# Moving the S5 rotation phases from GpSimd to ScalarE and VectorE in a two-layer SSD/S5 kernel

## The reference, cut to what matters

```python
for i in range(DEPTH):                       # DEPTH = 2
    u = rmsnorm(h, mix_norm_w[i])
    mix = ssd_mixer(u, ...) if i % 2 == 0 else s5_mixer(u, ...)
    h = h + mix
    h = h + conv_ffn(rmsnorm(h, ffn_norm_w[i]), ...)     # up 1024->5632, 3 taps, silu*val, down 2816->1024
    h = h + per_layer_embed(h, p[i], ...)                # (p @ w_proj) * sigmoid(rmsnorm(h) @ w_gate)
return rmsnorm(h, final_norm_w)
```

```python
step = jnp.exp(log_step[d])[:, None]
mag = jnp.exp(lr * step)
ang = li * step
lb_re = mag * jnp.cos(ang)
lb_im = mag * jnp.sin(ang)
```

## Time and profile before

| | |
|---|---|
| median of 3 runs | 1598.86 us (1595.52 to 1599.97) |
| the profiled execution | 1595.06 us |
| its span, first to last instruction | 1593.3 us |
| TensorE busy | 1517.2 us, 95% |
| VectorE busy | 1177.2 us, 74% |
| ScalarE busy | 725.6 us, 46% |
| GpSimd busy | 242.8 us, 15% |
| mean granted TensorE clock | 0.971 |

### The profile page before, as it was taken

How to read it: one execution, slowest core, us unless ns; L and a number is a source line. 1 busy time by engine, 2 the same in 40 slices (tenths; PEclk the granted TensorE clock), 3 DMA queues, 4 the chain that set the end, 5 groups by cost and what they waited for, 6 DMA issues and landing times.

```text
span 1593.3 us, 20269 instructions
## 1 busy us (share of the span) xinstructions
PE 1517.2 (95%) x7383; PEld 1233.8 (77%) x7383; DVE 1177.2 (74%) x1362; ACT 725.6 (46%) x1104; POOL 242.8 (15%) x244
## 2 busy tenths in 40 slices
PE   7989999999989999999998979989999999999998
PEld 5757767777677788888876759988888888888886
DVE  5687768678787989979899878974676666743354
ACT  4554454545634555224445451423355555532244
POOL 0154212020116600030057110000100000001001
PEclk9989999999999999999999995979999999999999
DMA  4334225234214433543335587932323323323222
GB/s 142 86 122 133 80 66 160 66 124 138 83 53 93 130 112 127 203 154 119 132 106 204 185 304 240 314 90 93 96 89 95 103 92 101 110 86 99 86 93 86
DMA packets 192234, 199.01 MB, mean 125 GB/s; under 512 B 47886, under 2 KB 178526, under 8 KB 188062
## 3 DMA queue, kind: packets, MB, share of 16 engines
q1 hardware_dynamic: 184510, 192.76, 38.1%
q10 hardware_dynamic: 7648, 5.25, 1.1%
HBM read 169.47 MB, written 28.51 MB: 124 GB/s over the span
## 4 chain that ended last, share of the span: by engine, by line
PE 72%; DVE 17%; issue 5%; DMA 2%; ACT 2%; SPq 0%; POOL 0%; DVEq 0%; ACTq 0%
PE ring L2111 21%; PE ring L2121 21%; PE ring L2112 21%; DVE w_lo L1483 2%; DVE rb L1893 2%; PE ring L2377 1%; DVE cc L1605 1%; PE pe_s L2397 1%; PE ring L2262 1%; DMA w_raw<-in_ssd_w_out 1%; DVE ytmp L1779 1%; DVE zs L1785 1%; DVE fwd L1643 1%; PE pe_s L2132 1%; ACT w_hi L1050 1%
## 5 line engine op out<-in xcount | busy, mean ns | idle before, releaser
L2111 PE MATMUL ring<-uh,w_hi 128*128 128x512 f32 x1160 | 458.8, 395 | 11.6 <-DVE cc L1605 3.7
L2112 PE MATMUL ring<-ul,w_hi 128*128 128x512 f32 x1160 | 453.8, 391 | 0.0
L1050 ACT ACTIVATE w_hi<-w_raw 128x1024 fp32r<-128x1024 f32 (+1 forms) x233 | 239.5, 1028 | 434.1 <-PE ring L2112 347.2
L1483 DVE TENSOR_TENSOR w_lo<-w_raw,w_hi 128x1024 fp32r<-128x1024 f32 (+1 forms) x233 | 287.5, 1234 | 163.6 <-PE ring L2121 139.8
L2121 PE MATMUL ring<-uh,w_lo 128*128 128x512 f32 x1160 | 288.7, 391 | 6.3 <-DVE w_lo L1483 6.3
L2111 PEld LDWEIGHTS ring<-uh,w_hi 128*128 128x128 f32 x1160 | 218.9, 189 | 64.2 <-issue 10.7
L2121 PEld LDWEIGHTS ring<-uh,w_lo 128*128 128x128 f32 x1160 | 218.0, 188 | 53.5 <-DVE w_lo L1483 7.8
L2112 PEld LDWEIGHTS ring<-ul,w_hi 128*128 128x128 f32 x1160 | 218.8, 189 | 47.2 <-issue 1.6
L2111 PE MATMUL ring<-gh,w_hi 128*128 128x512 f32 x480 | 189.2, 394 | 4.1 <-ACT w_hi L1050 2.8
L2112 PE MATMUL ring<-gl,w_hi 128*128 128x512 f32 x480 | 188.1, 392 | 0.0
L1992 DVE SCALAR_TENSOR_TENSOR cc<-cin,par,cc 128x512 f32<-128x512 f32 x176 | 129.6, 799 | 1.0 <-ACT cc L1406 1.0
(11 more groups left out here) (343 smaller groups left out, 2038.2 us busy)
## 6 DMA issues: line engine op xcount, KB each, us to landing
w_raw<-in_ffn_w_up SPq DMA_DIRECT2D x88, 512.0 KB, 3.5
w_raw<-in_ffn_w_down SPq DMA_DIRECT2D x40, 512.0 KB, 3.4
w_raw<-in_ssd_w_in SPq DMA_DIRECT2D x32, 512.0 KB, 3.8
s_tables<-tab SPq DMA_DIRECT2D x16, 1024.0 KB, 4.7
slot<-s_tables SPq DMA_DIRECT2D x16, 1024.0 KB, 7.3
fwd<-log_decays SPq DMA_DIRECT2D x16, 512.0 KB, 5.0
w_raw<-in_ssd_w_out SPq DMA_DIRECT2D x16, 512.0 KB, 3.5
w_raw<-in_ple_w_gate SPq DMA_DIRECT2D x16, 512.0 KB, 3.5
```

The source lines that it names most:

```text
L1050: act.activation(w_hi[u % 2][:, 0:n], w_raw[:, u % 2, 0:n], ACT.Copy).then_inc(hi_done, 1)
L1483: dve.tensor_tensor(w_lo[u % 2][:, 0:n], w_raw[:, u % 2, 0:n], w_hi[u % 2][:, 0:n].bitcast(F32), ALU.subtract).then_inc(lo_done, 1)
L2111: pe.matmul(o, wh[:, k, c], rh[:, k0 + k, :], start=first and k == 0, stop=False)
L2112: mm_ = pe.matmul(o, wh[:, k, c], rl[:, k0 + k, :], start=False, stop=False)
```

## The change

The four GpSimd steps of a turn are replaced. ScalarE makes the phase, eight scaled copies of the 64 multiples, one per group (128x64 each, the scale read from a column), and then adds the rounding constant in one 128x512 Identity with a bias column. VectorE subtracts the constant and the phase in one scalar_tensor_tensor of 128x512, which gives the difference with its sign turned; the sine's scale is negated for that. On ScalarE the turns of a round stand between the round's `hi_to` and its `squares`; the sines follow one round later, and the last two stand behind the square root. SyncE's saves of the turns stand behind D7, D8, D10, D11, then two behind P1, and the rest as before. Apart from that, the low half of F4 in the first pair of both FFNs is made ahead of its taps.

```diff
--- before.py
+++ after.py
@@ -279,7 +279,7 @@
         turn_at = [turn_a[:], turn_b[:], cin[:, :, 2:2 + SEQ], cc[:, 2:4, :],
                    ffn0[2][:].rearrange("p b n -> p (b n)").rearrange("p (a n) -> p a n", a=2)]
         turn_at += turn_at[0:3]
-        steps_row, quarter = tri[:, 0, 0:NCH], tri[:, 1, 0:1]
+        steps_row, quarter, magic = tri[:, 0, 0:NCH], tri[:, 1, 0:1], tri[:, 1, 1:2]
         bq_tmp = ct[:, 0]
         pv = ct[:, 1].rearrange("p g h -> p (g h)").rearrange("p (a n g) -> p a n g", a=2, n=LC)
         pv_tmp = ct[:, 0].rearrange("p g h -> p (g h)")[:, 0:(LC - 1) * S5G].rearrange("p (n g) -> p n g", g=S5G)
@@ -746,7 +746,7 @@
                                 saved = ({0: 1, 4: 2, 5: 3, 8: 4, 10: 5}, {2: 10, 7: 11, 10: 12})[part].get(n * i + kg)
                                 if saved is not None:
                                     save_table(saved)
-                                turned = {5: 0, 6: 1, 8: 2, 9: 3, 11: 4}.get(part * (n * i + kg))
+                                turned = {7: 0, 8: 1, 10: 2, 11: 3}.get(part * (n * i + kg))
                                 if turned is not None:
                                     turn_save(turned)
                 u = U[("ple", layer)]
@@ -763,6 +763,7 @@
                             proj_load(i)
                         if layer == 0:
                             if (i, kg) == (0, 0):
+                                turn_save(4)
                                 turn_save(5)
                             if (i, kg) == (0, 1):
                                 turn_save(6)
@@ -951,32 +952,13 @@
             def s5_steps():
                 pool.memset(tri[:, 0, 0:1], 0.0).then_inc(steps_done, 1)
                 pool.memset(quarter, PI / 2.0).then_inc(steps_done, 1)
+                pool.memset(magic, ROUND_MAGIC).then_inc(steps_done, 1)
                 for n in range(6):
                     w = 1 << n
-                    pool.wait_ge(steps_done, n + 2)
+                    pool.wait_ge(steps_done, n + 3)
                     pool.tensor_scalar(tri[:, 0, w:2 * w], tri[:, 0, 0:w], float(w), None, ALU.add, ALU.bypass
                                        ).then_inc(steps_done, 1)
-                pool.wait_ge(steps_done, 8)
-
-            def s5_turns(n):
-                if n < 2:
-                    pool.wait_ge(unit_done, U[("up", 0, 1)])
-                elif n < 4:
-                    pool.wait_ge(f_gl, HT + 2)
-                elif n == 4:
-                    pool.wait_ge(filled, FILL[("p", 0)] + PK)
-                else:
-                    pool.wait_ge(t_saved[n - 5], 16)
-                x, r = (turn_at[n][:, a].rearrange("p (g k) -> p g k", g=GB) for a in range(2))
-                pool.tensor_tensor(x, steps_row.unsqueeze(1).to_broadcast([P, GB, NCH]),
-                                   v5[:, V_F, GB * n:GB * n + GB].unsqueeze(2).to_broadcast([P, GB, NCH]), ALU.mult
-                                   ).then_inc(t_step, 1)
-                pool.wait_ge(t_step, 4 * n + 1)
-                pool.tensor_scalar(r, x, ROUND_MAGIC, None, ALU.add, ALU.bypass).then_inc(t_step, 1)
-                pool.wait_ge(t_step, 4 * n + 2)
-                pool.tensor_scalar(r, r, -ROUND_MAGIC, None, ALU.add, ALU.bypass).then_inc(t_step, 1)
-                pool.wait_ge(t_step, 4 * n + 3)
-                pool.tensor_tensor(r, x, r, ALU.subtract).then_inc(t_step, 1)
+                pool.wait_ge(steps_done, 9)
 
             def cut_rows(n):
 
@@ -1016,12 +998,8 @@
             pool.wait_ge(pv_done, 8)
             s5_order(ptv, lambda rows, a: pv[rows, a], ptv_done, (1.0, 1.0))
             pool.wait_ge(ptv_done, 4)
-            for n in range(5):
-                s5_turns(n)
             for m in range(1, KD - 2):
                 add_square(2, m)
-                if m in (1, 3, 5):
-                    s5_turns(5 + m // 2)
             for m in range(1, KD - 2):
                 add_square(3, m)
             pool.wait_ge(unit_done, U[("ple", 0)] + 12)
@@ -1381,14 +1359,32 @@
                 std(1 + 3 * layer)
                 if layer == 0:
 
+                    def turns(n):
+
+                        if n == 0:
+                            act.wait_ge(steps_done, 9)
+                            act.wait_ge(unit_done, U[("up", 0, 1)])
+                        elif n == 2:
+                            act.wait_ge(f_gl, HT + 2)
+                        elif n == 4:
+                            act.wait_ge(filled, FILL[("p", 0)] + PK)
+                        elif n > 4:
+                            act.wait_ge(t_saved[n - 5], 16)
+                        x, r_ = (turn_at[n][:, a] for a in range(2))
+                        for g in range(GB):
+                            act.activation(x[:, NCH * g:NCH * g + NCH], steps_row, ACT.Copy,
+                                           scale=v5[:, V_F, GB * n + g:GB * n + g + 1]).then_inc(t_step, 1)
+                        act.wait_ge(t_step, (GB + 1) * n + GB)
+                        act.activation(r_, x, ACT.Identity, bias=magic).then_inc(t_step, 1)
+
                     def sines(n):
 
                         x, r_ = (turn_at[n][:, a] for a in range(2))
-                        act.wait_ge(t_step, 4 * n + 4)
+                        act.wait_ge(steps_done, 9 + n + 1)
                         act.activation(x, r_, ACT.Abs).then_inc(t_abs, 1)
                         act.wait_ge(t_abs, n + 1)
                         act.activation(x, x, ACT.Sin, scale=-TURN, bias=quarter).then_inc(t_sin, 1)
-                        act.activation(r_, r_, ACT.Sin, scale=TURN).then_inc(t_sin, 1)
+                        act.activation(r_, r_, ACT.Sin, scale=-TURN).then_inc(t_sin, 1)
 
                 r = 2 + 3 * layer
                 for part, (first, pairs) in enumerate(parts):
@@ -1436,17 +1432,23 @@
                     for i in range(4):
                         hi_to(u + n * i + n + 1)
                         if part == len(parts) - 1:
+                            if layer == 0:
+                                turns(2 * i)
+                                turns(2 * i + 1)
                             if (layer, i) == (0, 0):
                                 act.wait_ge(tab_op, 6 * NB)
                             for m in (2 * i, 2 * i + 1):
                                 squares(r, m)
                                 u_hi(r, m, UH[layer])
-                            if layer == 0:
-                                sines(2 * i)
-                                sines(2 * i + 1)
+                            if layer == 0 and i:
+                                sines(2 * i - 2)
+                                sines(2 * i - 1)
                 u = U[("ple", layer)]
                 hi_to(u + 2)
                 std(r)
+                if layer == 0:
+                    sines(6)
+                    sines(7)
                 for i in range(4):
                     hi_to(u + GATE[i] + 3)
                     if layer == 1 and i >= 2:
@@ -1980,8 +1982,7 @@
                             for j in range(2):
                                 dve.tensor_tensor(cin[:, j, 2:2 + SEQ], bank(t + 2 * half + j), rstd[:], ALU.mult
                                                   ).then_inc(evac, 1)
-                            if not mixed:
-                                lo(u + 2 * half + 3, at=i * 4)
+                            lo(u + 4 if mixed else u + 2 * half + 3, at=i * 4)
                             for tap in range(1, 3):
                                 for j in range(2):
                                     if tap == 1:
@@ -1994,7 +1995,8 @@
                                                              scalar=dcol(i * 2 + (C_FCW + c)), in1=cc[:, 2 * half + j, :],
                                                              op0=ALU.mult, op1=ALU.add).then_inc(f_taps, 1)
                             if half == 0:
-                                lo(u + 4, at=i * 4)
+                                if not mixed:
+                                    lo(u + 4, at=i * 4)
                                 tables(more and more - 1)
                         for j in range(2):
                             dve.wait_ge(f_silu, i * 2 + (done + j + 1))
@@ -2043,6 +2045,12 @@
                         if part == len(parts) - 1:
                             for m in (2 * i, 2 * i + 1):
                                 u_lo(r, m, UH[layer], UL[layer])
+                            if layer == 0:
+                                for b in (2 * i, 2 * i + 1):
+                                    x, r_ = (turn_at[b][:, a] for a in range(2))
+                                    dve.wait_ge(t_step, (GB + 1) * (b + 1))
+                                    dve.scalar_tensor_tensor(out=r_, in0=r_, scalar=-ROUND_MAGIC, in1=x, op0=ALU.add,
+                                                             op1=ALU.subtract).then_inc(steps_done, 1)
 
                 u = U[("ple", layer)]
                 lo_to(u + 2)
```

## The result

The changed kernel takes 1627.63 us (median of 4 runs, 1621.28 to 1628.22) against 1599.41 before (4 runs, 1595.52 to 1600.34): ratio 1.0168, 95% interval 1.0146 to 1.0190, **28 us slower**. The prediction was 1622, range 1606 to 1633.

A forecast was written before the change was run, and what follows sets the result against it. TensorE, 95% busy, was taken as the bound, so edits count only through its waits. 23.7 + 1 = 24.7 us on 1595.06 gave 1619.8, 1623.6 with the median's 3.8; it said 1622, range 1606 to 1633.

The forecast's parts named there:

- Round 0 gains: With GpSimd's turns gone, D3's wait goes: at most 6.4 us of idle and some 2 us of slow clock back.
- ScalarE's block: Turns, squares, high halves and sines on ScalarE take 11.4 us a round instead of 5.9, uncovered in later rounds.
- The exposed loads: SyncE's loads for D8, D11, P2, P3 wait behind saves; a full load takes 4.6 us, a half one 3.6.
- TensorE's waits: Waits for high halves: some 8 us before D8, 6 to 8 before D11, 9 before P2, 6 before P3.
- P3's high half: At the PLE, done at 908.4 against 884.66 before, 23.7 us later; the order behind it is the old one.
- two signs of being wrong: Wrong if ScalarE reaches D8's high half before 846, or if D8's load is issued before 842.
- The table load ahead of sine 6: A second table load on ScalarE, back to the sine behind the square root, costs 1.28 us.
- F4: First FFN, low half ahead of the taps: the wait moves to F5, +1 us, between -3 and +3.
- B: Rival: blocks lengthen but loads are found in time, saves not holding them; +11 us, 1609; chance 0.11.
- C: Rival: blocks hide in ScalarE's waits, only VectorE's relief is left; 8 us less, 1591 or 1587; chance 0.09.
- D: Rival: the gain and the cost balance, 1599 us; chance 0.05.
- E: Rival: saves right ahead of loads stretch these to 6 us and more, with slow clock; +35, 1634; chance 0.07.

The follow-up runs named there:

- e7: The kernel before with GpSimd's four steps of a turn replaced by one fill, phases not computed: 1591.42 us, ratio 0.9958.
- e1: The changed kernel with every save of a turn one weight load later in SyncE's queue: 1616.52 us, ratio 1.0085 to the kernel before.
- e4: The kernel before, GpSimd's turns kept, only sines and saves reordered as in the change: 1615.61 us, ratio 1.0087.
- e5: The changed kernel with F4's low half behind its taps again: 1625.63 us, ratio 1.0163 to the kernel before.
- e6: The kernel before with only F4's low half moved ahead of its taps: 1601.89 us, ratio 1.0018.
- e2: The changed kernel with a turn's eight scaled copies replaced by one copy of another tensor, phases not computed: 1618.53 us, ratio 1.0103 to the kernel before.
- e8: The kernel before with turns 2 and 3 made by ScalarE and VectorE in round 0, turn 4 held until D3's low half: 1597.90 us, ratio 0.9991.
- e10: e8 with the saves of e9, one weight load later: 1596.45 us, ratio 0.9975 to the kernel before.
- e9: The kernel before with only its saves of turns one weight load later: 1600.11 us, ratio 1.0000.

## Why the prediction was right

Term by term, with the forecast first.

- **Round 0 gains.** D3's wait and its slow clock gone: so measured. The table steps take 1.22 us again (822.73), where they took up to 2.33, and a new step takes 0.68; I had 0.8. e7 puts the relief's whole worth at 6 to 8 us; I had 8. But the two turns didn't quite fit into round 0: they end at 829.0, and `h` was ready some 0.9 us earlier.
- **ScalarE's block.** I took 0.24 us a copy and 2.75 a turn; the trace has eight copies in 2.0 us and 2.67 a turn. The block of a later round was 11.4; in round 1 it runs from 840.6 to 851.9, 11.3.
- **The exposed loads.** I took 3.6 for a half load and 4.6 for a full one; the chain has 3.6 to 3.9 for D8 and D11, and 4.3 and 5.2 for P2 and P3. The other full loads on the chain took 4.0 (D7), 5.4 (D10) and 3.6 (P1), so the five full ones make 22.5 us against my 23.0: each was off by up to 1 us, and it is luck that the errors cancel. e1 removes the exposure, e4 makes it with no turn on ScalarE.
- **TensorE's waits.** Forecast 8 before D8, 6 to 8 before D11, 9 before P2, 6 before P3; measured 6.9, 5.95, 7.3, 4.5. D8's is shorter because its high half came 1.2 us earlier than forecast. Behind it I took no account of the slow clock in the units between, which turns part of an idle time into slow work: P2 took 7.8 us, not 5.4.
- **P3's high half** 23.7 us later, the term on which the sum stood; measured 911.4 - 884.7 = 26.7, less the 3.6 by which D0 began later, 23.1. On the same footing the high halves of D8 and P2 ended at 851.1 and 895.5, forecast 852.3 and 896.8. The stretch as a whole is 24.1 longer; the last 1 us comes behind P3's high half, 0.6 of it because P3 itself, at half clock, took 8.4 us and VectorE had to wait for it to take the tiles; I had about 8 and no wait. Of the two signs of being wrong neither came: ScalarE was ready for D8's high half at 851.9, not before 846, and D8's load was issued at 850.52, not before 842.
- **The table load ahead of sine 6** came, 1.28 us. It starts 0.02 us after the instruction before it ends (901.52 + 0.61 to 902.15), and the next one starts 0.02 us after it ends (903.43 to 903.45), so no drain lies around it. The Trainium skill ("ScalarE: Activation LUTs", What ACT_TABLE_LOAD costs) adds a drain of about 1.4 us to each switch; the trace doesn't show one here.
- **F4** +1 (-3 to +3): 1.5 to 1.8 in the traces, 2.0 and 2.5 in medians (e5, e6). Mis-sized a little: the taps took 9.9 us beside GpSimd, where I had kept the 8.2 of before, so F5 waited 5.8 us and not 4.8.

The parts balance roughly: order 16.6 (e4), relief -6.2 (e7), which leaves 24.1 - 16.6 + 6.2 = 13.7 for the rest of the change. This is a difference, not a measurement, and takes it that the parts add; no run has all the turns on ScalarE with the old order. Three blocks longer by 5.4 would be 16.2, and e2's slope (8.8 for 7.8) agrees that they aren't hidden. VectorE's new steps are in the same rest: they stand once on the chain, 1.3 us in round 0 ahead of D7's load. The rivals fall: B (loads found in time) by e1 and e4, C (relief is all that is left) and D (the two balance) by the result, E's stretched loads by the chain, where the longest took 5.4 us and the four behind a save 3.6 to 5.2, none 6.

What is left is the distance from 1622 to 1627.6. Of it, 1.6 lies between the sum, 1623.6, and the 1622 that I said; F4 beyond its +1 gives 0.5 to 1.5 and the stretch beyond its 23.7 gives 0.4. In the changed kernel's profile the eight S5 drives lie 94.0 us apart from first to last, 90.8 before; but in e5 to e8 and e10 they lie 90.6 to 91.6 apart and in e1 to e4 and e9 93.1 to 95.9, whatever was edited. TensorE waits there for the Toeplitz loads, 2.4 us before, 3.3 in the changed kernel and 4.7 in e9, but e10 has 3.2 of it with its drives 91.6 apart, so this isn't all. Why these executions differ stays open; I did not try it.

## What to carry to other kernels

Ask of a store in a queue that also carries prefetches what it waits for, and where that stands on the other engine: here a save whose data came just ahead of the consumer's next load left that consumer waiting 2.2 to 4.8 us, four times, and with the saves one place later the kernel was 11 us faster. Work moved off a contended engine pays only where the engine that takes it really waits: ScalarE was 46% busy, but it had waited 7.8 us for `h` in one round and 2.7, 1.9 and 1.0 in the next three, where a block grew by 5.4. A wait removed by hoisting one step can reappear at whatever stood behind it (here F4's at F5), so follow the list to the next consumer before counting a gain.

## What the hardware showed that I had not expected

A tap of 128x512 on VectorE took 9.90/4 = 2.5 us beside GpSimd's 128x1024 steps in the changed kernel and 2.06 in the one before. This isn't scatter: the four took 9.89 to 9.91 us in all five kernels with F4's low half ahead of them, and 8.24 in all seven without. So what GpSimd's steps cost the same four instructions depended on when these started beside them. VectorE's timeline of the changed kernel (start, us, of all four together):

```profile
514.45 9.90 DVE L1993 SCALAR_TENSOR_TENSOR cc<-cin,par,cc 128x512 f32<-128x512 f32 x4
```

Two executions of kernels that are the same up to there reached D0 at 804.8 (e8) and 810.3 us (e10), so a single profile's span says little about a gain of 4 us; stretch lengths from a common start did.
